# The gate-table products of the experts, issued as two each on the two halves of the array's columns

## The chip, the cores and the metric

The kernel runs on one core of one Trainium2 chip. The metric is the time of one execution of the whole program on the device, in microseconds (us); lower is better.

## The reference

Two transformer blocks are computed for 256 tokens of width 1024, in float32. The change lies in the last part of the second block, a product-key expert layer:

```python
def peer_ffn(x, w_query, keys_1, keys_2, expert_down, expert_up):
    # 8 heads, 128 x 128 = 16384 experts; each head picks 16 experts of every token
    ...
    gates = jax.nn.softmax(top_score, axis=-1)
    ...
        u = jnp.take(expert_down, ei, axis=0)
        act = jax.nn.gelu(jnp.einsum("btd,bthkd->bthk", xi, u), approximate=False)
        vv = jnp.take(expert_up, ei, axis=0)
        return jnp.einsum("bthk,bthkd->btd", gi * act, vv)
```

Each token has 8 x 16 = 128 picked experts with one gate each.

## The kernel before

**Units.** All weights stream in as 457 units of 128 x 1024 numbers (`raw`, four buffers, DMAs issued by SP). ScalarE (ACT) rounds each unit to its high part `WH`, VectorE (DVE), with GpSimd (POOL) on some units, computes the low part `WL`, and TensorE (PE) multiplies each 128 x 128 block three times (high x high, high x low, low x high) in the type float32r.

**The expert layer.** It doesn't gather experts. It computes gelu(u_e . x) for all 16384 experts and all 256 tokens in the 128 units `DN` to `DN + 127` (201 to 328), and keeps the results in `ACTS`. Each of these units is 24 float32r products with 128 x 128 weights and 256 moving columns (`products`). Then the 128 units `UP` multiply gate x gelu with the other expert table.

**The gate table.** The gates of a token form a 128 x 128 table (first key index x second key index). It is built on PE: for token t a product of a one-hot matrix of the first indices (`HOT`, 128 picks x 128 columns, the stationary side) with a one-hot matrix of the second indices scaled by the gates (`VG`, 128 picks x 128 columns, the moving side). This is a product of plain float32, not of float32r. There are 256 of them, in 64 groups g of four tokens. Each group fills one PSUM bank (2 or 7 in turn), four times 128 columns on 128 partitions.

**The order around them.** Every engine has a `Clock` that ticks four times in each unit, and side programs that start at a given tick. `build_side` on PE issues the four products of group g in one go, right behind the first tick of unit `BUILD + g` (255 + g). Ahead of product j it waits for `vgA` (g, j), that is for ACT to have written `VG[j]`; behind it it signals `buP` (g, j). `buP` (g, j) is what ACT waits for ahead of writing `VG[j]` of group g + 1, and `buP` (g, 3) is what DVE waits for ahead of the fold (multiply the bank into `ACTS`) and ahead of reusing `HOT` four groups on. ACT copies the rest of the bank to `ACTS` behind the fold (`fiA`), and PE waits for `fiA` (g - 2) ahead of group g.

**Where else TensorE uses part of its array.** `compress_side` multiplies float32 weights of 30 columns (output on 30 partitions) in small groups between the streaming products. `scores` (attention) multiplies with 64 contraction rows, alternately on rows 0 to 63 and 64 to 127, the two into different banks. `gates_side` multiplies float32r weights of 16 columns.

**Helpers.** Nearly all products are issued by the one line 675 (`mm`), so the profile's groups are told apart by tiles and shapes: `bank<-misc,xw`, `bank<-ones,xw` and `bank<-ident,xw` of 128x128 are the gate-table products (the four `VG` lie in `misc`, `misc`, `ones` and `ident`, and `HOT` in `xw`).

Of the kernel before, what the change touches and what calls it, by code (L numbers as in the profile page):

```python
# [38 lines left out]
def lo_share(u):  # L39

    if 10 <= u < 39:
        return 448
    if 39 <= u < 43:
        return 256
    if 115 <= u < 124 and u not in (121, 122):
        return 320
    if 124 <= u < 128 or 148 <= u < 171:
        return 384
    if QU + 2 <= u < DN + 2:
        return 320  # L50
    return 384 if DN + 2 <= u < DN + 50 else 0
# [67 lines left out]
def flat(x):  # L119
    return x.rearrange("p a b -> p (a b)")  # L120
# [11 lines left out]
def half(tile):  # L132
    return slice(128 * tile, 128 * tile + 128)


def program(nc, I, out):
    F32 = mybir.dt.float32
# [6 lines left out]
    with ExitStack() as ctx:  # L144
# [20 lines left out]
        VG = [misc[:, 900:1028], misc[:, 1028:1156], ones[:, :], ident[:, :]]  # L165
# [134 lines left out]
        HOT = [flat(XW[:, 2 * r:2 * r + 2, :]).rearrange("p (t n i) -> p t n i", n=2, i=128) for r in range(4)]  # L300
# [213 lines left out]
        buP = steps("build_pe", [(g, j) for g in range(NB) for j in range(4)])  # L514
# [45 lines left out]
        with nc.Block() as block:  # L560
# [110 lines left out]
            def _(e):  # L671
                clock = Clock()

                def mm(o, a, b, first=True, last=True):
                    return e.matmul(o, a, b, start=first, stop=last, skip_group_check=True)  # L675

                def lo_ready(u):
                    e.wait_ge(*lo.at(u))
                    if lo_share(u):
                        e.wait_ge(*lop.at(u))  # L680
# [47 lines left out]
                def products(u, o, xh, xl, k0=0, first=True, last=True):  # L728


                    wh, wl = WH[:, u % RW, :], WL[:, u % RW, :]
                    nk = 8 if o.shape[-1] == T else 4
                    n = 0
                    for g in range(8 // nk):
                        t = o[:, T * g:T * g + T]
                        for k in range(nk):
                            c = half(k * 8 // nk + g)
                            if n == 0:
                                if first:
                                    bank_ready(u)  # L740
                                e.wait_ge(*hi.at(u))
                            if g == 0:
                                high_ready(u, k)
                            mm(t, wh[:, c], xh[:, k0 + k, :], first and n == 0, False)
                            if g == 0:
                                low_ready(u, k)
                            mm(t, wh[:, c], xl[:, k0 + k, :], False, False)
                            if n == 0:
                                lo_ready(u)
                            z = mm(t, wl[:, c], xh[:, k0 + k, :], False, last and k == nk - 1)  # L750
                            n += 1
                            if n == 8:
                                z.then_inc(*unit.sent(u))
                            if n % 2 == 0:
                                yield

                def two_products(units, xh, xl):

                    for k in range(8):
                        c = half(k)  # L760
                        for u in units:
                            o = banks[bank_of(u)][:, 0:T]
                            wh, wl = WH[:, u % RW, c], WL[:, u % RW, c]
                            if k == 0:
                                bank_ready(u)
                            if u < 2 and k % 4 == 0:
                                e.wait_ge(*hi.at((u, k // 4)))
                            elif k == 0:
                                e.wait_ge(*hi.at(u))
                            high_ready(u, k)  # L770
                            mm(o, wh, xh[:, k, :], k == 0, False)
                            low_ready(u, k)
                            mm(o, wh, xl[:, k, :], False, False)
                            if u < 2 and k % 4 == 0:
                                e.wait_ge(*lo.at((u, k // 4)))
                            elif k == 0:
                                lo_ready(u)
                            z = mm(o, wl, xh[:, k, :], False, k == 7)
                            if k == 7:
                                z.then_inc(*unit.sent(u))  # L780
                        if k % 2:
                            yield

                def by_token(u):

                    if u == TM:
                        e.wait_ge(*evD.at(6))
                    e.wait_ge(*hi.at(u))
                    for kk in range(2):
                        k = 2 * (u - TM) + kk  # L790
                        w = slice(512 * kk, 512 * kk + 512)
                        for tile in range(2):
                            o = banks[(2, 0)[tile]][:, :]
                            a, b = XH[:, k, half(tile)], XL[:, k, half(tile)]
                            mm(o, a, WH[:, u % RW, w], k == 0, False)
                            mm(o, b, WH[:, u % RW, w], False, False)
                            if kk == 0 and tile == 0:
                                lo_ready(u)
                            z = mm(o, a, WL[:, u % RW, w], False, k == 7)
                            if kk == 1 and tile == 1:  # L800
                                z.then_inc(*unit.sent(u))
                            yield
# [399 lines left out]
                def build_side():  # L1202
                    for g in range(NB):
                        yield from clock.until(BUILD + g, 0)
                        b = banks[(2, 7)[g % 2]]
                        if g == 0:
                            e.wait_ge(*evA.at(DN + 45))
                        if g > 1:
                            e.wait_ge(*fiA.at(g - 2))
                        for j in range(4):  # L1210
                            e.wait_ge(*vgA.at((g, j)))
                            mm(b[:, half(j)], HOT[g % 4][:, j, 0, :].bitcast(F32), VG[j]).then_inc(*buP.sent((g, j)))

                clock.sides += [bias_side(), compress_side(), compressed_side(), attention_side(), mlp_stat_side(), gates_side(),
                                delta_side(), residual_side(), topk_side(), build_side()]
                for units in SLOTS[:-1]:
                    u = units[0]
# [1468 lines left out]
```

## Time and profile before

| what | value |
|---|---|
| time before, median of 3 runs | 1586.18 us (1585.17 to 1587.28) |
| the profiled execution's own time | 1586.05 us |
| its span, first to last instruction | 1584.2 us |
| mean granted TensorE clock | 0.988 of full |
| PE busy | 1531.3 us (97% of the span) |
| DVE / ACT / POOL busy | 1028.0 / 836.2 / 351.3 us |
| gate-table products | 960.4 to 1198.4 us, 512 records |

PE is the time in matmuls and PEld the time in loading stationary weights, which overlaps PE. The profiler's records of matmuls overlap too, since the array is pipelined: what a product costs in a stream is read from the distance of the starts, not from the duration. A float32 product shows as two matmul records and two weight loads, a float32r product as one of each. In the timeline, neighbours of one form are merged into one row: start, time from the first start to the last end, count.

### The profile page before, as it was taken

To read this page: it belongs to the slowest core of one execution; us is meant where nothing else is said; L and a number is where in the kernel's file an instruction comes from. 1 tells how busy PE (TensorE), PEld (TensorE's weight loads), DVE (VectorE), ACT (ScalarE), POOL (GpSimd) and SP (SyncE) were. 2 spreads that over 40 slices of the span, in tenths; PEclk is the share of its full clock that TensorE was granted. 3 is DMA by queue.
4 is the path that set the end of the run, shared out by engine and by line. 5 is a ranking of instruction groups with operands and counts; after the bars stand their busy time and mean duration, and the time that the engine had idled before them with its cause. 6 is when DMAs were issued, how large, how long until landed. Compare 5 with 4: busy or idle time off the path is not lost.

```text
span 1584.2 us, 28579 instructions
## 1 busy us (share of the span) xinstructions
PE 1531.3 (97%) x11138; PEld 1437.0 (91%) x11138; DVE 1028.0 (65%) x1792; ACT 836.2 (53%) x1638; POOL 351.3 (22%) x403
## 2 busy tenths in 40 slices
PE   7799999999988989999999999999999999999998
PEld 6389999999988989999999999999999888888886
DVE  4255567555576875476999976777775555555554
ACT  4166455444456543445444457777775554545454
POOL 1133431000155463321465540001112000000000
PEclk9899999999998999999999999999999999999999
DMA  9732455555433442356445554444444656666664
GB/s 216 224 107 81 133 184 169 178 183 186 160 108 113 146 139 77 106 168 195 147 159 174 174 184 151 146 136 145 137 144 162 196 191 196 189 197 194 192 196 137
DMA packets 76771, 254.20 MB, mean 160 GB/s; under 512 B 11375, under 2 KB 15293, under 8 KB 76509
## 3 DMA queue, kind: packets, MB, share of 16 engines
q1 hardware_dynamic: 76397, 251.71, 49.9%
q8 instruction: 90, 1.47, 0.4%
q0 software_dynamic: 240, 0.66, 0.2%
q14 instruction: 44, 0.36, 0.1%
HBM read 250.23 MB, written 1.84 MB: 159 GB/s over the span
## 4 chain that ended last, share of the span: by engine, by line
PE 80%; DVE 12%; DMA 2%; ACT 2%; POOL 2%; issue 1%; SPq 1%; POOLq 0%; DVEq 0%; ACTq 0%
PE bank L675 78%; DVE wl L1661 4%; DVE big L1661 2%; POOL big L2341 2%; DMA big<-in_w1k 1%; ACT big L1236 1%; DVE big L1664 1%; ACT wh L1236 1%; DVE big L2187 1%; DVE big L2198 1%; DVE big L2194 1%; DVE big L2183 1%; DVE big L2204 1%; DVE big L2191 1%; PE bank L984 1%
## 5 line engine op out<-in xcount | busy, mean ns | idle before, releaser
L1661 DVE TENSOR_TENSOR wl<-raw,wh 128x1024 fp32r<-128x1024 f32 (+4 forms) x459 | 531.5, 1159 | 399.5 <-ACT wh L1236 398.9
L1236 ACT ACTIVATE wh<-raw 128x1024 fp32r<-128x1024 f32 (+1 forms) x459 | 482.2, 1053 | 351.3 <-PE bank L675 333.1
L675 PE MATMUL bank<-gw,wh 128*128 128x256 f32 x3504 | 651.3, 287 | 2.4 <-DVE big L1664 2.4
L675 PEld LDWEIGHTS bank<-gw,wh 128*128 128x128 f32 x3504 | 547.4, 193 | 3.0 <-DVE big L1664 2.8
L675 PE MATMUL bank<-gw,wl 128*128 128x256 f32 x1752 | 497.7, 284 | 6.4 <-POOL wl L2341 5.0
L675 PEld LDWEIGHTS bank<-gw,wl 128*128 128x128 f32 x1752 | 336.8, 192 | 8.0 <-issue 6.3
L675 PE MATMUL bank<-xw,wh 128*128 128x256 f32 x1696 | 321.9, 290 | 9.9 <-ACT wh L1236 7.5
L675 PE MATMUL bank<-wh,xw 128*128 128x512 f32 x1056 | 326.9, 391 | 0.0
L675 PEld LDWEIGHTS bank<-xw,wh 128*128 128x128 f32 x1696 | 267.9, 194 | 16.8 <-ACT wh L1236 7.8
L1236 ACT ACTIVATE big<-bank 128x256 f32<-128x256 f32 (+23 forms) x326 | 118.5, 373 | 260.6 <-PE bank L675 222.7
L2341 POOL TENSOR_TENSOR wl<-raw,wh 128x384 fp32r<-128x384 f32 (+3 forms) x131 | 175.6, 1346 | 336.9 <-ACT wh L1236 336.9
L675 PE MATMUL bank<-xw,wl 128*128 128x256 f32 x848 | 242.3, 286 | 1.1 <-POOL wl L2341 1.1
L675 PEld LDWEIGHTS bank<-wh,xw 128*128 128x128 f32 x1056 | 197.0, 188 | 46.0 <-issue 5.8
L675 PE MATMUL bank<-wl,xw 128*128 128x512 f32 x528 | 205.5, 389 | 0.0
L675 PEld LDWEIGHTS bank<-xw,wl 128*128 128x128 f32 x848 | 164.3, 194 | 2.1 <-DVE wl L1661 2.1
L2341 POOL TENSOR_TENSOR big<-big 128x256 f32<-128x256 f32 (+15 forms) x124 | 105.6, 862 | 222.0 <-ACT big L1236 185.6
L675 PE MATMUL bank<-big 128*128 128x128 f32 (+8 forms) x848 | 122.6, 297 | 17.6 <-DMA big<-in_w1k 12.0
L675 PEld LDWEIGHTS bank<-big 128*128 128x128 f32 (+3 forms) x848 | 97.3, 185 | 31.3 <-issue 24.8
L675 PEld LDWEIGHTS bank<-wl,xw 128*128 128x128 f32 x528 | 99.1, 188 | 20.6
L2341 POOL TENSOR_TENSOR big<-big,cols 128x8 f32<-128x8 f32 (+2 forms) x13 | 13.2, 1014 | 363.9 <-DVE big L2329 347.4
L2341 POOL TENSOR_TENSOR big<-big,misc 128x256 f32<-128x256 f32 (+32 forms) x74 | 37.1, 501 | 251.1 <-ACT misc L1236 251.1
L1661 DVE TENSOR_TENSOR big<-big 128x256 f32<-128x256 f32 (+4 forms) x143 | 75.9, 543 | 20.7 <-ACT big L1236 14.4
(136 smaller groups left out, 1107.7 us busy)
## 6 DMA issues: line engine op xcount, KB each, us to landing
raw<-in_wst SPq DMA_DIRECT2D x455, 512.0 KB, 3.6
big<-toeplitz SPq DMA_DIRECT2D x8, 256.0 KB, 14.2
big<-in_w1k SPq DMA_DIRECT2D x4, 512.0 KB, 18.1
big<-in_w1v SPq DMA_DIRECT2D x4, 512.0 KB, 19.4
big<-in_xT SPq DMA_DIRECT2D x4, 256.0 KB, 5.0
raw<-in_wst SPq DMA_DIRECT2D x4, 256.0 KB, 4.7
big<-in_keys SPq DMA_DIRECT2D x1, 1024.0 KB, 5.5
out<-big SPq DMA_DIRECT2D x4, 256.0 KB, 2.4
```

Source lines behind the costliest of these rows:

```text
L675: return e.matmul(o, a, b, start=first, stop=last, skip_group_check=True)
L984: z = e.transpose(b[:, half(m)], S[s % 6][:, m // (tile + 1), half(m % (tile + 1))], ident[:, :])
L1236: return e.activation(o, x, f, **kw)
L1661: return e.tensor_tensor(o, a, b, f)
L1664: return e.scalar_tensor_tensor(o, a, s, b, f, g)
L2183: e.max(v[:, 0:8], s).then_inc(*tkD.sent((h, tile, names[0][k])))
L2187: e.match_replace(x, v[:, 0:8], s, -3.0e38).then_inc(*tkD.sent((h, tile, names[1][k])))
L2191: e.max(v[:, 8:16], x).then_inc(*tkD.sent((h, tile, names[2][k])))
L2194: e.max_index(i[:, 0:8], v[:, 0:8], s).then_inc(*tkD.sent((h, tile, names[3][k])))
L2198: e.max_index(i[:, 8:16], v[:, 8:16], x).then_inc(*tkD.sent((h, tile, names[4][k])))
L2204: e.tensor_reduce(p[:, :, h, :], flat(room).rearrange("p (t k i) -> p t k i", t=2, i=16), AX, ALU.add).then_inc(*tkD.sent((h, "red", n)))
L2341: return e.tensor_tensor(o, a, b, f)
```

## The change

Each of the 256 gate-table products is issued as two: columns 0 to 63 of the stationary matrix into partitions 0 to 63 of the bank, then columns 64 to 127 into partitions 64 to 127, both with the same 128 moving columns. The wait for `vgA` stays ahead of the first, the signal `buP` stays behind the second.

```diff
+                def columns(o, a, b):
+
+                    for r in (slice(0, 64), slice(64, 128)):
+                        z = mm(o[r, :], a[:, r], b)
+                    return z
...
                         for j in range(4):
                             e.wait_ge(*vgA.at((g, j)))
-                            mm(b[:, half(j)], HOT[g % 4][:, j, 0, :].bitcast(F32), VG[j]).then_inc(*buP.sent((g, j)))
+                            columns(b[:, half(j)], HOT[g % 4][:, j, 0, :].bitcast(F32), VG[j]).then_inc(*buP.sent((g, j)))
```

## Rows read from the trace of the kernel before

**Rows 1.** The profile's page: span, busy time, granted clock by slices.
```profile
span 1584.2 us, 28579 instructions
PE 1531.3 (97%) x11138; PEld 1437.0 (91%) x11138; DVE 1028.0 (65%) x1792; ACT 836.2 (53%) x1638; POOL 351.3 (22%) x403
PEclk9899999999998999999999999999999999999999
```
**Rows 2.** The chain of work that ended last, 940 to 1210 us.
```profile
940.00 270.11 PE bank L675 x2290
```
**Rows 3.** Busy time of the engines: the stretch of the gate table, and the compress stretch.
```profile
core 0: us, PE busy (x) PEld busy (x) DVE busy (x) ACT busy (x) POOL busy (x), PEclk, DMA share, GB/s
56.00:82.00 26.00, 26.00 (x110) 12.05 (x109) 4.42 (x20) 5.99 (x12) 5.58 (x4) 1.00 0.43 155
960.40:1201.60 241.20, 241.20 (x2051) 241.20 (x2051) 176.00 (x191) 182.40 (x508) 29.16 (x64) 1.00 0.44 141
```
**Rows 4.** Instructions on the tile xw, engine PE, 955 to 1205 us.
```profile
L675 PE MATMUL bank<-misc,xw x256: 272/274/275, 960.4 to 1198.0; 128*128 128x128 f32 x128
L675 PE MATMUL bank<-ones,xw x128: 275/275/275, 960.8 to 1198.2; 128*128 128x128 f32 x128
L675 PE MATMUL bank<-ident,xw x128: 275/275/275, 961.0 to 1198.4; 128*128 128x128 f32 x128
```
**Rows 5.** Timeline of PE around one group: start, length, what, count.
```profile
1050.63 0.28 PE L675 MATMUL bank<-gw,wl 128*128 128x256 f32 x1
1050.75 0.61 PE L675 MATMUL bank<-misc,xw 128*128 128x128 f32 x4
1051.20 0.39 PE L675 MATMUL bank<-ones,xw 128*128 128x128 f32 x2
1051.42 0.39 PE L675 MATMUL bank<-ident,xw 128*128 128x128 f32 x2
1051.57 0.48 PE L675 MATMUL bank<-gw,wh 128*128 128x256 f32 x2
1051.89 0.28 PE L675 MATMUL bank<-gw,wl 128*128 128x256 f32 x1
1052.01 0.40 PE L675 MATMUL bank<-gw,wh 128*128 128x256 f32 x2
1052.24 0.28 PE L675 MATMUL bank<-gw,wl 128*128 128x256 f32 x1
...
1054.52 0.61 PE L675 MATMUL bank<-misc,xw 128*128 128x128 f32 x4
```
**Rows 6.** Timeline of PE: products with 30 stationary columns between full ones.
```profile
56.17 1.05 PE L675 MATMUL bank<-big 128*30 128x256 f32 x4
57.15 0.72 PE L675 MATMUL bank<-wh,xw 128*128 128x512 f32 x2
57.71 0.40 PE L675 MATMUL bank<-wl,xw 128*128 128x512 f32 x1
58.04 1.05 PE L675 MATMUL bank<-big 128*30 128x256 f32 x4
...
59.91 1.05 PE L675 MATMUL bank<-big 128*30 128x256 f32 x4
```
**Rows 7.** The last two of four such records, and their durations.
```profile
56.62 0.59 PE L675 MATMUL bank<-big 128*30 128x256 f32 x2
L675 PE MATMUL bank<-big x69: 272/379/402, 56.2 to 81.8; 128*30 128x256 f32 x53, 64*128 64x128 f32 x16
```
**Rows 8.** Busy time in a stretch of float32r products with 512 columns alone.
```profile
1250.00:1300.00 50.00, 50.00 (x222) 41.41 (x221) 29.13 (x37) 24.76 (x37) 0.00 (x0) 1.00 0.61 197
```
**Rows 9.** Timeline of PE: attention scores on 64 rows each, between full products.
```profile
117.31 0.28 PE L675 MATMUL bank<-xw,wl 128*128 128x256 f32 x1
117.52 1.13 PE L675 MATMUL bank<-big 64*128 64x256 f32 x8
118.59 0.51 PE L675 MATMUL bank<-xw,wh 128*128 128x256 f32 x2
118.93 0.28 PE L675 MATMUL bank<-xw,wl 128*128 128x256 f32 x1
```
**Rows 10.** The last four of these eight records, and their durations.
```profile
118.06 0.60 PE L675 MATMUL bank<-big 64*128 64x256 f32 x4
L675 PE MATMUL bank<-big x8: 376/376/480, 117.5 to 118.3; 64*128 64x256 f32 x8
```
**Rows 11.** Timeline of PE: float32r products with 16 stationary columns.
```profile
453.38 0.28 PE L675 MATMUL bank<-xw,wl 128*128 128x256 f32 x1
453.50 0.85 PE L675 MATMUL bank<-xw,gw 128*16 128x256 f32 x6
454.18 0.40 PE L675 MATMUL bank<-xw,wh 128*128 128x256 f32 x2
454.42 0.28 PE L675 MATMUL bank<-xw,wl 128*128 128x256 f32 x1
```
**Rows 12.** Timeline of PE: full weights with one moving column.
```profile
20.01 0.95 PE L675 MATMUL bank<-ones,big 128*128 128x1 f32 x8
20.82 0.48 PE L675 MATMUL bank<-xw,wh 128*128 128x256 f32 x2
```

## The prediction

> **What bounds the kernel now.** I read the page first, then the chain that ended last, then the busy time of the stretch that the change touches, then PE's timeline record by record. On the page PE is busy for 97% of the span [rows 1]. In the stretch of the gate table the chain is one piece of PE alone: 270 us with no other engine in it [rows 2]. There PE is busy for 241.2 of 241.2 us, while DVE has 176.0, ACT 182.4 and the DMA engines 44% [rows 3]. So whatever PE's instruction stream gets longer or shorter by in these 64 units goes straight into the time, and the other engines have room on both sides.
>
> What the stream costs is read from starts. One period, from group to group, is 1054.52 - 1050.75 = 3.77 us [rows 5]. In it the float32r products with 256 columns follow each other at 0.12 us: from 1050.63 (`wl`) to 1051.89 (the next `wl`) lie one such product, the eight records of the group and two more products, 1.26 us in all, less 3 x 0.12 leaves **0.90 us for the group**, 0.112 us for each of its eight records. Check: 24 x 0.12 + 0.90 = 3.78 us, the period. There are 64 groups: 512 records from 960.4 to 1198.4 us [rows 4]. All gate-table products together take 64 x 0.90 = 57.6 us, 3.6% of the time.
>
> **The change, part by part.** It removes 512 matmul records with 128 stationary columns and as many weight loads, and adds 1024 with 64 columns. No wait is added and no signal moved: the wait for `vgA` still stands ahead of the first half, `buP` behind the second, so nothing new is queued behind a wait. Three costs follow.
>
> *1. What a record costs.* In a float32 record a moving column costs the same whatever the stationary width: the 30-column products with 256 moving columns stand 0.59 - 0.379 = 0.21 us apart [rows 7], so 128 columns take half, some 0.108 us. The loading of 128 stationary columns alone takes 0.10 us or more: eight records with one moving column fill 20.82 - 20.01 = 0.81 us [rows 12]. A half's load should need half of that and hide behind its matmul. So a record costs between 0.108 (streaming) and 0.112 us (as today); it doesn't become cheaper because its weights are narrower.
>
> *2. Whether the two halves run at the same time.* No row here has two column halves. The nearest is the attention's scores, which use two row halves of the array: four records from 118.06 take 0.60 us of which the last lasts 0.376, so they are two pairs, 0.22 us apart [rows 10]; one record of this kind with 256 columns takes 0.21 us by itself. Two halves thus run wholly in parallel, and eight records take four slots. The bounds are: in parallel, 8 slots x 0.108 to 0.112 = 0.86 to 0.90 us a group; one after the other, 16 x 0.108 = 1.73 us. I take 0.88, by the row of the row halves: the records of the column halves are of the same type, and independent in the same way. What differs is that both halves read the same 128 partitions of `VG` and write one bank, on other partitions.
>
> *3. Entering and leaving the partial array.* The 30-column products show it. Their period is 58.04 - 56.17 = 1.87 us, and the next is the same, 59.91 - 58.04 [rows 6]. It holds three float32r products with 512 columns at 50.00 / 222 = 0.225 us [rows 8] and four records at 0.216 (twice 0.108): 0.68 + 0.86 = 1.54. The rest, **0.32 to 0.33 us, is lost at the two ends**, where no weights can be loaded ahead. The row halves with full loads of 128 columns show the upper bound: from 117.31 to 118.93 are 1.62 us [rows 9], less three products at 0.12 and four slots at 0.216 leaves 0.40. Between 30 and 128 stationary columns the loss grows by 0.07 us, so at 64 columns I take 0.35. It is paid once per group, since all eight half products stand together: 64 times.
>
> Of this loss the Trainium skill has the rule, in "TensorEngine Tiling (Array Packing)", Key Properties: changing the tiling mode drains TensorE, changing only the tile doesn't. The trace agrees that each visit costs; the page has no figure. The same skill, in "TensorE: Matmul & The Clock Gate", Measured speedup vs the span model, gives 2.38 times for three column tiles, 79% of full overlap. By that rate the eight slots would take about 1.1 us rather than 0.88 (an estimate), and the sum would come to about 1621 us.
>
> **The sum.** Per group 0.35 + 0.88 - 0.90 = +0.33 us; 64 x 0.33 = **+21.1 us**. The profiled execution took 1586.05 us in all (span 1584.2 plus 1.85 around it), the median is 1586.18, so its rows need no scaling: 1586.2 + 21.1 = **1607 us**, 1.3% slower. The bounds of this case: 0.32 + 0.86 - 0.90 = 0.28 gives +18 (1604); 0.40 + 0.90 - 0.90 = 0.40 gives +26 (1612).
>
> Costed at nothing: the signals reach ACT and DVE 0.15 to 0.35 us later after the group's start, but each unit is 0.33 longer, and ACT has 241 - 182 = 59 us of idle time in the stretch, some 0.9 us a unit; without that room `VG` of the next group would hold PE. The 1024 additional matmul and weight-load records are fetched ahead, and hide behind the matmuls of 0.1 us. DMA runs at 44% of its share; the weights come a little slower per us, which takes from nobody. Nothing behind the stretch gets the time back: the `UP` units follow on PE itself.
>
> **The rivals.**
>
> *The two halves run one after the other.* Both read the same partitions at the same moment, which the row halves never do, and no row here shows two column tiles at once. Then a group takes 0.35 + 1.73 = 2.08 us, +1.18, 64 times +75.5: **1662 us**. Against it: the row halves overlap to within 0.01 us a pair [rows 10], and the array is addressed in the same way. 14%.
>
> *They overlap, but not throughout.* If PE keeps the order first half (two records), second half (two records), only the second record of one half meets the first of the next: one slot more a group, +0.11, 1614 us. If the slot at either end is unshared, +0.22, +14 in all: **1621 us**. This is also the size that the skill's rate for column tiles gives. Against it: in rows 10 the records pair up although each product is two records there as well. 12%.
>
> *There is no loss at the ends.* The 16-column products pay none: from 453.38 to 454.42 lie nine records, 1.04 us, 0.115 each [rows 11]. If float32 products of 64 columns went the same way, and overlapped, a group would take 0.86 to 0.90: -0.04 to 0 us, -2.6 to 0 us in all: **1584 to 1586 us**, not slower. It decides if the loss is under 3.2 / 64 = 0.05 us a group. Against it: the 16-column ones are float32r, and the 30-column ones are float32, like the changed ones, and pay. 4%.
>
> *The clock falls.* The added gaps could lower the granted clock from 2.4 to 1.2 GHz in part of the stretch; every us at the lower level costs up to half a us. Against it: in 56 to 82 us the array works on 30 of 128 columns for half of the time, with two such gaps in 1.87 us, and the granted clock is 1.00 [rows 3]; here there would be one visit in 4.1 us. 2%.
>
> **How the numbers follow.** Parallel halves with the loss at the ends 68% (1604 to 1612, likeliest 1607), partial overlap 12% (1614 to 1621), serial 14% (1662), no loss 4% (1584 to 1586), clock 2%. A range of 1602 to 1622 holds the first two, 80%: the lower end is 1604 less the rounding of the rows (0.01 us in three terms, 64 times, is 2 us), the upper end is the partial overlap. A measurement of this kernel tells about 0.2% from no change, 3.2 us. Faster by more: 1% for the third rival (its whole gain is under 3.2 us) and 1% for what I don't see; within 0.2%: 3%, from the third rival; slower: 95%.
>
> **What the profile after would show.** Right: 1024 records of 128*64 for the gate-table products; between groups a period of about 4.10 us in place of 3.77 [rows 5]; the stretch of 64 units about 21 us longer; PE still alone in the chain and never waiting for `VG`; a gap of about 0.09 us (as 117.52 - 117.31 less 0.12 [rows 9]) ahead of the first half product and of the next full one, each with a weight load that nothing hides; the starts of two halves within 0.01 us. Wrong: pairs 0.1 us apart throughout and a period near 4.95 us (serial); no gap at the ends (no loss); a granted clock under 1.00 between 960 and 1220 us; or PE waiting for ACT, which would mean that the room of the other engines was misread.

## The result and the profile after

The changed kernel takes 1608.35 us (median of 4 runs, 1605.99 to 1610.47) against 1586.49 us for the kernel before in the same comparison: 1.0142 times, 95% interval 1.0130 to 1.0154, or 22 us slower. The forecast was 1607 us.

The page of the kernel after, lines that answer to [rows 1]:
```profile
span 1606.9 us, 29603 instructions
PE 1554.9 (97%) x11650; PEld 1442.3 (90%) x11650; DVE 1028.6 (64%) x1792; ACT 836.1 (52%) x1638; POOL 349.8 (22%) x403
PEclk9899999999998999999999999999999999999999
```
PE has 512 more matmul records (11650 for 11138) and 23.6 us more busy time; the work of the other engines is the same to within 2 us, and the clock line is the same digit for digit.

Its chain of waits from 940 to 1230 us, and the busy time of the stretch (us, then busy time and count for PE, PEld, DVE, ACT, POOL, the clock, the share of the DMA engines, GB/s), to be read against [rows 2, 3]:
```profile
939.94 290.17 PE bank L675 x2795
```
```profile
960.40:1222.00 261.60, 261.60 (x2559) 242.12 (x2558) 177.09 (x191) 182.73 (x509) 28.93 (x63) 1.00 0.38 131
```
Still one piece of PE, and never idle by these views. But PEld, the loading of weights, which filled 241.2 of 241.2 us before, now fills 242.1 of 261.6. This window is 20.4 us longer, and 19.5 us of it are time in which no weights are loaded.

The gate-table products by tile (count, durations in ns, first and last start), to be read against [rows 4]:
```profile
L675 PE MATMUL bank<-misc,xw x512: 272/273/324, 962.2 to 1220.4; 128*64 128x128 f32 x171
L675 PE MATMUL bank<-ones,xw x256: 272/273/273, 962.7 to 1220.7; 128*64 128x128 f32 x128
L675 PE MATMUL bank<-ident,xw x256: 272/273/273, 962.9 to 1220.9; 128*64 128x128 f32 x128
```
1024 records. From the first start in `misc` to the last are 258.2 us where they were 237.6: **+20.6 us over 63 periods, 0.327 us each**. The first one starts at 962.2 where it was 960.4. That 1.8 us lies ahead of all that was changed; in the profiles of the twelve experiments, whose programs compute the same up to there, this start lies between 955.4 and 961.7 us, so it belongs to the single execution. The granted clock is part of it: between 480 and 525 us it is 0.89 here and 0.96 in the run with 955.4.

The timeline of PE around one group, to be read against [rows 5]:
```profile
1052.03 0.28 PE L675 MATMUL bank<-gw,wl 128*128 128x256 f32 x1
1052.23 0.66 PE L675 MATMUL bank<-misc,xw 128*64 128x128 f32 x8
1052.72 0.39 PE L675 MATMUL bank<-ones,xw 128*64 128x128 f32 x4
1052.94 0.39 PE L675 MATMUL bank<-ident,xw 128*64 128x128 f32 x4
1053.26 0.51 PE L675 MATMUL bank<-gw,wh 128*128 128x256 f32 x2
1053.60 0.28 PE L675 MATMUL bank<-gw,wl 128*128 128x256 f32 x1
...
1056.33 0.33 PE L675 MATMUL bank<-misc,xw 128*64 128x128 f32 x2
```
From `wl` to `wl` are 1053.60 - 1052.03 = 1.57 us; less three ordinary products at 0.12 leaves 1.21 us for the group, where it was 0.90. The period is 1056.33 - 1052.23 = 4.10 us. Four records with `ones` take 0.39 us: before, two took the same 0.39 [rows 5]. So two halves cost what one whole product cost.

The weight loads of the same moment show what stands at the ends:
```profile
1051.91 0.19 PEld L675 LDWEIGHTS bank<-gw,wl 128*128 128x128 f32 x1
1052.23 0.42 PEld L675 LDWEIGHTS bank<-misc,xw 128*64 128x64 f32 x8
...
1052.83 0.25 PEld L675 LDWEIGHTS bank<-ident,xw 128*64 128x64 f32 x4
1053.26 0.30 PEld L675 LDWEIGHTS bank<-gw,wh 128*128 128x128 f32 x2 [0.17 <-issue]
```
In the ordinary stream a load starts 0.12 us ahead of its matmul. Here the first half's load starts with its matmul at 1052.23, and so does the first full one at 1053.26, behind 0.17 us in which nothing is loaded. The starts show where the loss lies: 0.08 us ahead of the first half product (1052.23 - 1052.03 - 0.12), 0.05 in the first four slots (1052.72 - 1052.23 = 0.49 for 0.44), 0.10 ahead of the next full product (1053.26, where the last of four slots from 1052.72 would end at 1053.16), and 0.10 behind it (1053.60 - 1053.26 = 0.34 for two products, 0.24 in the ordinary stream). Together 0.33 us, 0.13 on the way in and 0.20 on the way out. The starts of two halves lie within 0.01 us of each other.

### The profile page after: what moved, and what is told of

Read it like the earlier page. It is cut to its first block, busy times and chain, and to the rows that moved or that the text cites. A ratio compares the mean times of both kernels' runs of the same rounds, so it can differ in the third digit from the quotient of the medians.

```text
span 1606.9 us, 29603 instructions
## 1 busy us (share of the span) xinstructions
PE 1554.9 (97%) x11650; PEld 1442.3 (90%) x11650; DVE 1028.6 (64%) x1792; ACT 836.1 (52%) x1638; POOL 349.8 (22%) x403
## 4 chain that ended last, share of the span: by engine, by line
PE 80%; DVE 11%; DMA 2%; ACT 2%; POOL 2%; issue 1%; SPq 0%; POOLq 0%; DVEq 0%; ACTq 0%
PE bank L675 79%; DVE wl L1667 4%; DVE big L1667 2%; POOL big L2347 1%; DMA big<-in_w1k 1%; ACT big L1242 1%; DVE big L1670 1%; ACT wh L1242 1%; DVE big L2193 1%; DVE big L2204 1%; DVE big L2200 1%; DVE big L2189 1%; DVE big L2210 1%; DVE big L2197 1%; PE bank L990 0%
## 5 line engine op out<-in xcount | busy, mean ns | idle before, releaser
L675 PEld LDWEIGHTS bank<-wl,xw 128*128 128x128 f32 x528 | 99.1, 188 | 20.6
```

## The experiments

Twelve kernels, each timed against the kernel before on the same chip; the medians of the kernel before lie between 1584.57 and 1586.51 us, so a difference between two kernels of different comparisons is uncertain by some 2 us. A slot is the distance of two record starts on one half of the array, some 0.109 us. A visit is one stay of PE in the group's products, between ordinary ones.

| run | us (median) | ratio, 95% interval |
|---|---|---|
| two_visits_halves | 1628.85 | 1.0265 (1.0247 to 1.0282) |
| two_visits_whole | 1585.98 | 1.0002 (0.9992 to 1.0011) |
| same_tile | 1662.43 | 1.0484 (1.0466 to 1.0501) |
| first_half_only | 1605.87 | 1.0123 (1.0103 to 1.0144) |
| quarters | 1604.06 | 1.0119 (1.0097 to 1.0140) |
| moving_halves | 1643.26 | 1.0351 (1.0333 to 1.0368) |
| halves_apart | 1639.52 | 1.0338 (1.0320 to 1.0355) |
| every_second_group | 1595.54 | 1.0055 (1.0035 to 1.0074) |
| two_apart | 1609.94 | 1.0153 (1.0136 to 1.0170) |
| three_apart | 1624.38 | 1.0245 (1.0228 to 1.0262) |
| gate_fp32r | 1588.36 | 1.0012 (1.0001 to 1.0024) |
| gate_fp32r_four | 1558.55 | 0.9837 (0.9824 to 0.9850) |

### Is the cost one of visits or of products?

two_visits_halves, against the changed kernel (a tick of PE's clock lies between products 1 and 2):
```diff
                         for j in range(4):
+                            if j == 2:
+                                yield
                             e.wait_ge(*vgA.at((g, j)))
```


> The changed kernel with each group of four products issued in two visits of two products, one tick apart (64 groups, 128 visits of the half array). Theory: the loss belongs to the visit (two changes between the whole and the half array), 0.32 to 0.35 us each, so another 64 visits cost +20 to +22 us over the changed kernel: 1628 to 1631 us. Rival: the loss belongs to the half products themselves (their number is unchanged): 1608 us.

two_visits_whole is the same edit made on the kernel before.

> The kernel before with the same two visits of two whole products each, the control. Theory and rival alike: whole products change no mode, so 1586 to 1587 us. If the splitting of the group by itself cost something (a signal that comes later, a wait for it), it would show here as more than 1589 us.

Measured: 1628.85 us, 20.5 above the changed kernel, and 1585.98 for the control. The number of half products is the same, only the visits are doubled. The timeline of PE in two_visits_halves:
```profile
1049.79 0.28 PE L675 MATMUL bank<-gw,wl 128*128 128x256 f32 x1
1050.00 0.66 PE L675 MATMUL bank<-misc,xw 128*64 128x128 f32 x8
...
1050.93 0.28 PE L675 MATMUL bank<-gw,wl 128*128 128x256 f32 x1
```
`wl` to `wl` 1.14 us, less 0.36, is 0.78 us for a visit of four slots; a visit of eight takes 1.21. The difference, 0.43, is four slots of 0.108, and what is left of either visit is 0.35 us of loss.

every_second_group, against the changed kernel:
```diff
-                            columns(b[:, half(j)], ...
+                            (columns if g % 2 else mm)(b[:, half(j)], ...
```


> Only the groups with odd number are issued as halves, the others whole: 32 visits instead of 64. Theory: the cost is per visit and adds up without regard to the rest: half of +22 us, 1596 to 1598 us. Rival: something of the whole stretch (the clock, another engine that falls behind) sets the cost: nearer to 1586 or 1608 us.

Measured 1595.54 us, 0.5 below what was expected and 9.0 above the kernel before of its comparison, for 32 visits. The trace is sharper: from the first start in `misc` (959.0) to the last (1206.9) are 247.9 us, 10.3 more than before, 0.33 for each of the 31 half groups between them. With 32, 64 and 128 visits at +9, +22 and +43 us the cost goes with the visits, 0.28 to 0.34 us each. PE is alone in the chain in all three traces.

### Do the halves run at the same time, and why?

first_half_only, against the changed kernel:
```diff
-                    for r in (slice(0, 64), slice(64, 128)):
+                    for r in (slice(0, 64),):
                         z = mm(o[r, :], a[:, r], b)
```


> The changed kernel with the second half products left out (partitions 64 to 127 of the gate tables are left unwritten, the output is not the reference's). Theory: the second halves run beside the first and cost 0.007 us a group, so leaving them out saves under 1 us: 1607 to 1608 us. The whole +22 us stays although half of the product work is gone. Rival: the second halves cost stream time of their own (partial overlap, 0.1 to 0.2 us a group): 1595 to 1602 us.

same_tile:
```diff
-                        z = mm(o[r, :], a[:, r], b)
+                        z = mm(o[0:64, :], a[:, r], b)
```


> The changed kernel with both halves written to partitions 0 to 63, so both use the same half of the array (the upper half of each gate table is left unwritten, the lower holds the second half's product: the output is not the reference's). Theory: the halves of the changed kernel run at the same time only because they lie on different halves of the array. On the same one a group takes 16 slots of 0.108 to 0.112 instead of 8: +0.86 to 0.90 us a group, +55 to +58 us, 1663 to 1666 us. Rival: two small products overlap wherever they lie: 1608 us.

Measured: 1605.87 and 1662.43 us, the first 1.1 and the second 0.6 below the expected ranges. The first is 2.5 us under the changed kernel, more than the 1 us expected, but from another comparison, with runs from 1602.68 to 1608.32. The traces are sharper. PE's timeline in first_half_only:
```profile
1053.12 0.28 PE L675 MATMUL bank<-gw,wl 128*128 128x256 f32 x1
1053.33 0.65 PE L675 MATMUL bank<-misc,xw 128*64 128x128 f32 x4
...
1054.69 0.28 PE L675 MATMUL bank<-gw,wl 128*128 128x256 f32 x1
```
`wl` to `wl` 1.57 us: to the hundredth what it is with the second halves. The whole stretch of `misc` is 257.9 us (959.3 to 1217.2), against 258.2. And in same_tile:
```profile
1053.43 0.28 PE L675 MATMUL bank<-gw,wl 128*128 128x256 f32 x1
1053.64 1.09 PE L675 MATMUL bank<-misc,xw 128*64 128x128 f32 x8
...
1055.88 0.28 PE L675 MATMUL bank<-gw,wl 128*128 128x256 f32 x1
```
2.45 us, less 0.36, is 2.09: the loss of 0.35 and 16 slots of 0.109. The half products overlap because they lie on different halves of the array, and the overlap is complete. In same_tile the two also write the same addresses of the bank; that this isn't what keeps them apart is seen in first_half_only, where successive products lie on one half, write different addresses, and their records still start 0.11 us apart (1054.03 - 1053.82 for two). That both read the same partitions of `VG` and write the same bank costs nothing.

quarters:
```diff
-                    for r in (slice(0, 64), slice(64, 128)):
+                    for r in [slice(32 * i, 32 * i + 32) for i in range(4)]:
```


> The changed kernel with each product in four, on 32 stationary columns each, partitions 0, 32, 64 and 96. Theory: the four quarters run at the same time, 8 slots of 0.108 us a group as before, and the first weight load of a visit, which nothing hides, is 32 columns instead of 64, 0.02 to 0.03 us shorter: 1605 to 1608 us, 1 to 2 us under the changed kernel. Rival: only two column tiles run at once: 16 slots, +0.87 us a group, 1664 us.

Measured 1604.06 us. PE's timeline:
```profile
1053.15 0.28 PE L675 MATMUL bank<-gw,wl 128*128 128x256 f32 x1
1053.36 0.65 PE L675 MATMUL bank<-misc,xw 128*32 128x128 f32 x16
...
1054.71 0.28 PE L675 MATMUL bank<-gw,wl 128*128 128x256 f32 x1
```
And its products with `misc` by tile:
```profile
L675 PE MATMUL bank<-misc,xw x1024: 272/273/297, 955.4 to 1212.9; 128*32 128x128 f32 x171
```
Sixteen records in the time of four. The group takes 1.20 us for 1.21, and the stretch of `misc` 257.5 us for 258.2: 0.7 us in the whole, less than the 1 to 2 us expected of the shorter first load. The rest of the 4 us in the medians (0.9 below the expected range) isn't from there. The four runs spread from 1601.18 to 1607.87, and in the profiled one, the fastest, the first of these products starts at 955.4 us, 6.8 earlier than in the profile of the changed kernel, ahead of everything that differs.

### What bounds a record?

moving_halves, on whole weights, with the moving columns split:
```diff
                     for r in (slice(0, 64), slice(64, 128)):
-                        z = mm(o[r, :], a[:, r], b)
+                        z = mm(o[:, r], a, b[:, r])
```


> The kernel before with each product split the other way: both with all 128 stationary columns, each with 64 of the 128 moving columns. Theory: no change of mode and so no loss at the ends, but a record can't be shorter than its weight load of 128 columns (0.10 to 0.112 us), so 16 records take 1.8 instead of 0.9 us: +57 us, 1643 to 1645 us. Rival: a record costs its moving columns, 0.056 us with 64: 1586 us.

Measured 1643.26 us. Half of the moving columns make a record no shorter. PE's timeline:
```profile
1053.58 0.28 PE L675 MATMUL bank<-gw,wl 128*128 128x256 f32 x1
1053.70 1.00 PE L675 MATMUL bank<-misc,xw 128*128 128x64 f32 x8
1054.54 0.61 PE L675 MATMUL bank<-ones,xw 128*128 128x64 f32 x4
```
Eight records fill 1054.54 - 1053.70 = 0.84 us, 0.105 each with the shorter first one, and the whole change costs 56.8 us for 512 records, 0.111 each. It enters at once (0.12 from `wl` to the first), so whole weights don't pay the loss at the ends. What keeps a record with 64 moving columns at 0.11 us isn't shown: it can be the load of 128 stationary columns, as the expectation has it, or a floor that every float32 record has. Few stationary together with few moving columns were not tried.

### How far apart may the halves stand?

halves_apart, in place of the loop over j:
```diff
+                        for n in range(2):
+                            r = slice(64 * n, 64 * n + 64)
+                            for j in range(4):
+                                if n == 0:
+                                    e.wait_ge(*vgA.at((g, j)))
+                                z = mm(b[r, half(j)], HOT[g % 4][:, j, 0, r].bitcast(F32), VG[j])
+                                if n == 1:
+                                    z.then_inc(*buP.sent((g, j)))
```


> The changed kernel with the order within a group changed: the first halves of all four products, then the second halves of all four. The same work and the same visits. Theory: the overlap needs the two halves next to each other in PE's stream. With eight records of one half and then eight of the other only the records at the seam can overlap: 15 or 16 slots, +0.8 us a group, 1655 to 1663 us. Rival: PE picks ready work for each half of the array from its queue, however far apart: 1608 us.

Measured 1639.52 us. Neither the theory (1655 to 1663) nor the rival (1608) holds. PE's timeline; the first half's products are `misc`, `misc`, `ones`, `ident`, two records each, and then those of the second half in the same order:
```profile
1053.22 0.65 PE L675 MATMUL bank<-misc,xw 128*64 128x128 f32 x4
1053.71 0.27 PE L675 MATMUL bank<-ones,xw 128*64 128x128 f32 x1
1053.71 0.32 PE L675 MATMUL bank<-misc,xw 128*64 128x128 f32 x1
1053.82 0.27 PE L675 MATMUL bank<-ones,xw 128*64 128x128 f32 x1
1053.88 0.27 PE L675 MATMUL bank<-misc,xw 128*64 128x128 f32 x1
1053.93 0.27 PE L675 MATMUL bank<-ident,xw 128*64 128x128 f32 x1
...
1054.42 0.38 PE L675 MATMUL bank<-ident,xw 128*64 128x128 f32 x2
1054.73 0.50 PE L675 MATMUL bank<-gw,wh 128*128 128x256 f32 x2
```
The ninth record of the stream (the first `misc` of the second half) starts with the fifth, so it has passed the sixth to eighth, but it started no earlier. The two `ident` records that it passed are a whole product that stands ahead of it in the program, so this isn't only the two records of one product changing places. Two more orders test whether three is the reach. Each pair is (product, half); the body is that of halves_apart.

two_apart and three_apart:
```diff
# two_apart
+                        for j, n in ((0, 0), (1, 0), (0, 1), (1, 1), (2, 0), (3, 0), (2, 1), (3, 1)):
# three_apart
+                        for j, n in ((0, 0), (1, 0), (2, 0), (0, 1), (1, 1), (2, 1), (3, 0), (3, 1)):
```


> The changed kernel with the halves ordered by twos: first halves of products 0 and 1, then their second halves, then the same for 2 and 3. With all four apart the second half's first record (ninth in the stream) started together with the fifth of the first half, so it had passed three records, and a group took 12 to 13 slots. Theory: PE starts a record of the other half ahead of at most three or four that come before it. Here the first record of a second half is the fifth, with four at most ahead of it, so the halves overlap from the first slot or the second: 8 or 9 slots a group, 1608 to 1615 us. Rival: overlap needs neighbours and what was seen was the seam alone; then two seams a group would leave 12 slots or more, 1635 us or more.

> The changed kernel with the first halves of products 0, 1 and 2, then their second halves, then the two halves of product 3. Theory of the limited reach (three or four records): the first record of a second half is the seventh, so it starts with the third of the first half, two slots late; the six and the two of each half then end in about 10 slots: +0.22 us a group over the changed kernel, 1620 to 1624 us. If reach had no limit: 1608 us.

Measured 1609.94 us, inside what the theory gave, and 1624.38, 0.4 above it. Short windows of PE's timeline show which records have started. In two_apart two have by 1052.86 us, 0.03 behind the first start. In three_apart (1052.38 to 1052.42 us):
```profile
1052.17 0.43 PE L675 MATMUL bank<-misc,xw 128*64 128x128 f32 x2
```
With the second half's first record in fifth place it passes three and overlaps from the first slot. In seventh place it comes two slots late: up to 1052.42 us two records have started, and by 1052.46 two more, the third and the one from the other half.

What counts are the records in front that haven't started, not the distance. In quarters the first record of the fourth quarter is the seventh of the stream, and yet four records have started by 1053.45, 0.09 us after the first:
```profile
1053.36 0.32 PE L675 MATMUL bank<-misc,xw 128*32 128x128 f32 x4
```
It has passed the second, fourth and sixth, again three. Three records in front can be passed, in all these orders; what the count stands for inside PE was not tried.

### Is there a version that beats both?

The profile says what a group costs: eight records at 0.11 us, because a float32 product is two records. With float32r products it is one. gate_fp32r, against the kernel before:
```diff
-        VG = [misc[:, 900:1028], misc[:, 1028:1156], ones[:, :], ident[:, :]]
+        vgt = sb("vgt", [128, 384], F32R)
+        VG = [vgt[:, 128 * i:128 * i + 128] for i in range(3)]
...
-        mm(b[:, half(j)], HOT[g % 4][:, j, 0, :].bitcast(F32), VG[j])
+        mm(b[:, half(j)], HOT[g % 4][:, j, 0, :], VG[(4 * g + j) % 3])
...
-                            if g:
-                                e.wait_ge(*buP.at((g - 1, j)))
+                            if 4 * g + j > 2:
+                                e.wait_ge(*buP.at(divmod(4 * g + j - 3, 4)))
```


> The kernel before with its whole (128-column) gate-table products in float32r instead of float32, so the gates are rounded to float32r and a product is one record instead of two; its moving side lies in three buffers of a new tensor. Theory: a record with 128 columns each way costs its weight load, 0.112 us, whatever its type, and there is no change of mode, so a group takes 0.45 instead of 0.90 us: -29 us, 1557 to 1559 us. Rival: the shorter period of 3.33 us uncovers another engine (ACT has 182 us of work in the stretch, 2.85 us a unit, and one buffer fewer to run ahead): 1562 us or more.

Measured 1588.36 us: no gain, where 1557 to 1559 was expected; the rival was right. PE's timeline in gate_fp32r:
```profile
1052.00 0.45 PE L676 MATMUL bank<-vgt,xw 128*128 128x128 f32 x3
1052.71 0.33 PE L676 MATMUL bank<-vgt,xw 128*128 128x128 f32 x1 [0.27 <-ACT vgt L1237]
```
Its chain of waits at the same moment:
```profile
1052.26 0.41 ACT vgt L1237
1052.67 0.04 issue
1052.71 3.32 PE bank L676 x26
```
With three buffers ACT can write the fourth `VG` only when the first product of the same group is done; PE then waits for its 0.41 us. From `wl` (1051.88) to `wl` (1053.17) are 1.29 us, where they were 1.26: the saving of 0.45 us a group went into a new wait. gate_fp32r_four puts the fourth buffer back:
```diff
+        VG = [vgt[:, 128 * i:128 * i + 128] for i in range(3)] + [ones[:, :].bitcast(F32R)]
```


> The run with whole gate-table products in float32r (gates rounded to float32r) and three buffers for their moving side showed PE and ACT waiting for each other once a group: the fourth buffer could be written only when the first product of the same group was done, and the fourth product waited 0.4 us for it. Here the same with four buffers, as before. Theory: the wait alone took the gain; with four buffers ACT writes all four ahead, a group takes 4 x 0.112 = 0.45 instead of 0.90 us, -29 us: 1556 to 1560 us. Rival: it was float32r products with 128 columns, or ACT's total work (2.85 us of a unit of 3.33), that hold the stretch up: 1575 us or more.

Measured **1558.55 us, 0.9837 times the kernel before** (interval 0.9824 to 0.9850), 26 us faster than it and some 50 us faster than the changed kernel. Half products in float32r were not tried. PE's timeline:
```profile
1049.92 0.28 PE L676 MATMUL bank<-gw,wl 128*128 128x256 f32 x1
1050.04 0.45 PE L676 MATMUL bank<-vgt,xw 128*128 128x128 f32 x3
1050.33 0.27 PE L676 MATMUL bank<-ones,xw 128*128 128x128 f32 x1
1050.44 0.45 PE L676 MATMUL bank<-gw,wh 128*128 128x256 f32 x2
1050.73 0.28 PE L676 MATMUL bank<-gw,wl 128*128 128x256 f32 x1
```
`wl` to `wl` 0.81, less 0.36, is 0.45 us for the group. The gates are rounded to float32r in it; whether that is acceptable is for whoever owns the accuracy of the layer.

## Why the prediction was right

*The bound.* PE alone is the chain in the stretch, before and after, and all that its stream gained in length arrived in the time: 64 x 0.327 = 20.9 us in the trace.

*The cost of a record* was taken as 0.108 to 0.112 us, 0.88 for eight slots. Narrower weights didn't make it cheaper (first_half_only), fewer moving columns neither (moving_halves). The price read from the 30-column products [rows 7] fits the half products (0.109), and the one read from the records with one moving column [rows 12] fits moving_halves (0.111); that the second is the price of the load stays an inference, and the sum doesn't need it.

*The overlap of the halves*, taken from the row halves of the attention [rows 10], holds in full for column halves: 0.39 us for four records, the same with the second halves left out, and twice the slots when both lie on the same half of the array. The serial rival (1662) was wrong for this kernel and right to 1 us for same_tile. The rival of partial overlap fell too. The 79% that the Trainium skill's example gives ("TensorE: Matmul & The Clock Gate", Measured speedup vs the span model) isn't what this stream shows: here it was all of it. The overlap hangs on something that the prediction didn't have: PE starts a record of the other half ahead of up to three that stand before it. In the changed kernel only one has to be passed, so the assumption held with room to spare, but that the order of the stream matters came out in the experiments alone: with the halves six records apart the time is 1624, eight apart 1640.

*The loss at the ends* was interpolated to 0.35 us from 30 and 128 columns [rows 6, 9]. Measured: 1.21 - 8 x 0.109 = 0.34, with a gap of 0.08 us ahead of the first half product and of 0.10 ahead of the next full one (0.09 was forecast for each). The control without mode changes (two_visits_whole) shows no such loss, and doubled visits pay it twice. The Trainium skill's rule in "TensorEngine Tiling (Array Packing)", Key Properties, that a change of the tiling mode drains TensorE while a change of tile does not, agrees with this: two changes of mode cost 0.34 us, and the changes between the two halves inside a visit cost nothing. The rival without loss, drawn from the float32r products of 16 columns [rows 11], fell.

*The clock* stayed at 1.00 in the stretch. *The other engines* kept their room: none appears in the chain.

*The sum* of +21.1 us was measured as +20.9 in the trace of the stretch and +22 in the medians; the remaining 1 us is within the spread of single runs. The period came out at 4.10 us, as forecast.

## What to carry to other kernels

Part of the array is another mode of the array for these float32 products: a visit costs about 0.34 us here with four slots, eight or sixteen in it. So it can pay only where enough halves stand in one visit, and where they would otherwise leave the other half idle; no run here shows such a gain. Why the float32r products of 16 columns pay nothing [rows 11] was not tried. Splitting a product that already fills the array gains nothing, since its halves together cost what the whole did. Where PE is the only thing in the chain, count records and what each of them costs; and when a shorter stream brings nothing, look for the buffer that the freed time now waits for.

## What the runs showed of the hardware that was not expected

- PE lets a record of the other half of the array start ahead of three unstarted ones that stand before it in the stream, no more. With halves, it starts together with the first at a distance of two and of four records (1608 and 1610 us), two slots late at six (1624), four slots late at eight (1640); with quarters also at a distance of six, since there only three of those in front are unstarted. The Trainium skill says in "TensorE: Matmul & The Clock Gate", section The mechanism, that matmuls start strictly in program order and only weight loads are pulled ahead. The trace of halves_apart differs for these float32 products, and the measurement decides: a `misc` record that stands ninth starts at 1053.71, ahead of the sixth at 1053.82 and of the seventh (`ident`, another product) at 1053.93.
- Four column tiles of 32 run fully in parallel in float32: sixteen records start within the time of four (1053.36 to 1053.82 us in quarters, 0.46, against 0.49 with halves).
- Float32r products with 128 columns on either side cost 0.11 us a record, the same as one of the two records of a float32 product, so 0.45 us a group in place of 0.90.
